# A decoder trunk on one core: the sample tile of the odd layer's input projection as unrounded products of raw weight slices, at the start of its column chunk

## The reference

```python
xn = _rms(x, norm_g)
q, k, v, g_c, qi, wi, ki, xq, g_x = _split(xn @ w_in, ODD_SPLITS)
```

## Time and profile before

| | |
|---|---|
| median of 3 runs | 1839.22 us (1837.75 to 1840.47) |
| the profiled execution | 1835.88 us, span 1834.3 us |
| PE busy in the span | 1749.9 us (95%) |
| DVE, ACT, POOL busy | 978.5 us (53%), 601.0 us (33%), 412.7 us (23%) |
| mean granted clock of TensorE | 0.989 |
| DMA | 237.10 MB, mean 129 GB/s |

### The profile page before, as it was taken

How to read it: one execution, slowest core, us unless ns; L and a number is a source line. 1 busy time by engine, 2 the same in 40 slices (tenths; PEclk the granted TensorE clock), 3 DMA queues, 4 the chain that set the end, 5 groups by cost and what they waited for, 6 DMA issues and landing times. The chain is left out here.

```text
span 1834.3 us, 26510 instructions
## 1 busy us (share of the span) xinstructions
PE 1749.9 (95%) x9413; PEld 1352.0 (74%) x9413; DVE 978.5 (53%) x2277; ACT 601.0 (33%) x1271; POOL 412.7 (23%) x643
## 2 busy tenths in 40 slices
PE   6999999999999999998999999999999679999999
PEld 5666788777888887886876567887777456777887
DVE  5422653233677655212541667888879665774111
ACT  3110332111122113101211346787735445553010
POOL 4301221100143452000341001211005455420000
PEclk9999999999999999999999999999999899999999
DMA  6433342545566467122222121334343775241231
GB/s 215 132 108 117 123 118 101 165 137 155 181 176 193 135 221 299 75 96 73 80 71 77 42 75 65 117 100 146 129 146 115 253 225 162 85 131 66 101 121 46
DMA packets 134765, 237.10 MB, mean 129 GB/s; under 512 B 28550, under 2 KB 61222, under 8 KB 134634
## 3 DMA queue, kind: packets, MB, share of 16 engines
q1 hardware_dynamic: 111066, 172.48, 29.0%
q0 software_dynamic: 17184, 55.85, 9.4%
q10 hardware_dynamic: 6384, 7.08, 1.1%
HBM read 169.12 MB, written 66.17 MB: 128 GB/s over the span
## 5 line engine op out<-in xcount | busy, mean ns | idle before, releaser
L1282 PE MATMUL ring_acc<-ring_w_hi,layer_xT_hi 128*128 128x512 f32 x640 | 260.8, 407 | 0.2 <-PE all_banks L1432 0.2
L1284 PE MATMUL ring_acc<-ring_w_hi,layer_xT_lo 128*128 128x512 f32 x640 | 249.9, 391 | 0.0
L1283 PE MATMUL ring_acc<-ring_w_lo,layer_xT_hi 128*128 128x512 f32 x640 | 249.7, 390 | 0.0
L2869 PE MATMUL front_acc<-front_w_hi,front_xT_hi 128*128 128x512 f32 x520 | 218.6, 420 | 10.5 <-DVE front_w_lo L3410 5.2
L2871 PE MATMUL front_acc<-front_w_hi,front_xT_lo 128*128 128x512 f32 x520 | 205.7, 396 | 0.0
L2870 PE MATMUL front_acc<-front_w_lo,front_xT_hi 128*128 128x512 f32 x520 | 205.5, 395 | 0.0
L1282 PEld LDWEIGHTS ring_acc<-ring_w_hi,layer_xT_hi 128*128 128x128 f32 x640 | 120.3, 188 | 29.5 <-issue 6.6
L1284 PEld LDWEIGHTS ring_acc<-ring_w_hi,layer_xT_lo 128*128 128x128 f32 x640 | 120.1, 188 | 26.1
L1283 PEld LDWEIGHTS ring_acc<-ring_w_lo,layer_xT_hi 128*128 128x128 f32 x640 | 120.4, 188 | 25.4 <-issue 2.6
L2869 PEld LDWEIGHTS front_acc<-front_w_hi,front_xT_hi 128*128 128x128 f32 x520 | 98.6, 190 | 43.3 <-issue 11.8
L3195 ACT ACTIVATE front_index_rows<-odd_bias,front_candidate 128x1024 bf16<-128x1024 f32 (+3 forms) x128 | 124.9, 981 | 9.0 <-DVEq L3559 5.1
(11 more groups left out here) (715 smaller groups left out, 3585.6 us busy)
## 6 DMA issues: line engine op xcount, KB each, us to landing
all_w<-in_w_even POOLq DMA_DIRECT2D x80, 256.0 KB, 3.8
h_even<-layer_st SPq DMA_DIRECT2D x79, 256.0 KB, 2.1
all_w<-in_w_odd POOLq DMA_DIRECT2D x61, 256.0 KB, 3.5
h_odd<-front_st SPq DMA_DIRECT2D x55, 256.0 KB, 2.1
layer_scratch<-h_even SPq DMA_DIRECT2D x46, 256.0 KB, 3.0
all_scratch<-in_w_mem SPq DMA_DIRECT2D x32, 256.0 KB, 3.6
all_scratch<-h_even SPq DMA_DIRECT2D x32, 256.0 KB, 3.6
all_scratch<-x SPq DMA_DIRECT2D x14, 512.0 KB, 3.9
```

What stands on the lines that cost most here:

```text
L1282: T.matmul(out[0:rows, :], xh[:, kk, to], wh[:, r, :], start=(kk == 0), stop=False)
L1283: T.matmul(out[0:rows, :], xh[:, kk, to], wl[:, r, :], start=False, stop=False)
L1284: ins = T.matmul(out[0:rows, :], xl[:, kk, to], wh[:, r, :], start=False, stop=(kk == KC - 1))
L2869: T.matmul(out[0:rows, :], xh[:, k, to], wh[:, r, :], start=(k == 0), stop=False, skip_group_check=True)
```

## The change

In chunks 2 to 7 the sample tile is no longer made from the split weights. It is made from the raw slices and an unrounded fp32 copy of the sample rows (`x_smp`), as four products of 128 columns for each slice, each into its own group of 32 PSUM partitions, so that the tile is 128 x 128 and not 32 x 512. As only four slices are raw at a time, it is made in two halves. Slices 0 to 3 of the next chunk are taken in the middle of unit j = 3 of the chunk before, into the bank of the unit before it, and ACT copies that sum to `hold`. Slices 4 to 7 are taken in the unit j = 0 of the chunk itself; DVE adds the two halves. So the order of tiles in chunks 2 to 7 becomes sample, 0, ..., 7 (`ORDERS`). The loads of raw slices wait until the products have read them. Chunks 0 and 1 stay as they were.

```diff
+        ORDERS = [list(range(T1)), list(range(B - 1)) + [B, B - 1]] + [[B] + list(range(B))] * (len(ORDER) - UNROUNDED)
+        tile_at = lambda chunk, j: ORDERS[chunk][j]
+        in_parts = lambda n: n == 2 * T1 - 2
+        of_sample = lambda n: n >= UNROUNDED * T1 and n % T1 == 0
+        by_dve = lambda n: ORDER[n // T1][1] or in_parts(n) or of_sample(n)
...
 # POOL, load_w(q)
+                was, k = divmod(q - RAW, KC)
+                if was >= UNROUNDED:
+                    pool.wait_ge(*((smp_mm, was - UNROUNDED + 1) if k < RAW else (mm, T1 * was + 1)))
...
 # PE
+            def sample(chunk, part, out):
+                for k in range(RAW * part, RAW * part + RAW):
+                    from_, there = slice_in(KC * chunk + k)
+                    pe.wait_ge(*there)
+                    for g in range(4):
+                        ins = T.matmul(out[32 * g:32 * g + SMP, 0:P], x_smp[:, k, :], from_[:, P * g:P * g + P],
+                                       start=(k % RAW == 0), stop=(k % RAW == RAW - 1))
+                return ins
+
             def half(n, side):
...
                 if side == 0:
...
+                    if j == HALF_AT + 1 and UNROUNDED <= chunk + 1 < len(ORDER):
+                        pe.wait_ge(held, chunk + 1 - UNROUNDED + 1)
+                    if of_sample(n):
+                        sample(chunk, 1, out).then_inc(mm, 1)
...
+                elif j == HALF_AT and UNROUNDED <= chunk + 1 < len(ORDER):
+                    pe.wait_ge(*evacuated(n - 1))
+                    sample(chunk + 1, 0, psD[(n + 1) % 2]).then_inc(smp_mm, 1)
+                if of_sample(n):
+                    if (n, side) in second_pairs:
+                        next(pairs)
+                    return
...
-                    if j == 0:
+                    if j == (1 if chunk >= UNROUNDED else 0):
                         pe.wait_ge(split_d, q + 1)
...
 # ACT, dense(n)
+                if n % T1 == HALF_AT and UNROUNDED <= chunk + 1 < len(ORDER):
+                    if chunk >= UNROUNDED:
+                        act.wait_ge(*evacuated(T1 * chunk))
+                    act.wait_ge(smp_mm, chunk + 1 - UNROUNDED + 1)
+                    A(hold[:, :], psD[(n + 1) % 2][:, 0:P], ACT.Copy, scale=0.5 if ORDER[chunk + 1][1] else 1.0).then_inc(held, 1)
...
 # DVE, dense(n)
-                if in_parts(n) and ORDER[chunk][1]:
-                    acc = psD[n % 2][0:SMP, :]
-                    dve.wait_ge(parts, part(n))
-                    V.tensor_tensor(acc, acc, st_of(n)[0:SMP, :], ALU.add).then_inc(whole, 1)
+                if of_sample(n):
+                    acc = psD[n % 2][:, 0:P]
+                    dve.wait_ge(mm, n + 1)
+                    dve.wait_ge(held, chunk - UNROUNDED + 1)
+                    if ORDER[chunk][1]:
+                        V.scalar_tensor_tensor(acc, acc, 0.5, hold[:, :], ALU.mult, ALU.add).then_inc(whole, 1)
+                    else:
+                        dve.wait_ge(*stored_by(n - ST))
+                        V.tensor_tensor(st_of(n)[:, 0:P], acc, hold[:, :], ALU.add).then_inc(ev_v, 1)
```

More of the change, by code:

```diff
@@ L2382, in layer1_front @@
         Q = s.sb("index_rows", [P, 5 * TOK])
-        xh, xl = (s.sb(n, [P, KC, TOK + SMP], F32R) for n in ("xT_hi", "xT_lo"))
+        xh, xl = (s.sb(n, [P, KC, SEQ], F32R) for n in ("xT_hi", "xT_lo"))
         wh, wl = (s.sb(n, [P, RING, CW], F32R) for n in ("w_hi", "w_lo"))
+        xs_parts = s.sb("xT_smp_hi_lo", [P, KC, 2 * SMP], F32R)
+        x_smp, hold = s.sb("xT_smp", [P, KC, SMP]), s.sb("first_half", [P, P])
         raw = c.raw
@@ L2446, in layer1_front @@
             s.sem("evacuated_by_dve"), s.sem("tanhs"), s.sem("stored", ST))
-        parts, whole, ia_in = s.sem("sample_parts"), s.sem("sample_whole"), s.sem("idx_pages_by_act_in", PAGED)
+        smp_mm, held, whole, ia_in = s.sem("first_halves"), s.sem("first_halves_held"), s.sem("sample_whole"), s.sem("idx_pages_by_act_in", PAGED)
         x_in, small_in, wk_d, wkd, rope_in = (s.sem("x_in", 2), s.sem("small_in"),
@@ L2473, in layer1_front @@
         FIRST_TILES = (0, TILES)
-        BOTH = slice(SEQ, TOK + SMP)
+        UNROUNDED, HALF_AT = 2, 3
         def slice_in(q):
@@ L2484, in layer1_front, with tanhs_to @@
         st_of = lambda n: c.vals[1][:, 0, :] if n == UNITS - 1 else st[(n - T1) % ST]
-        tile_at = lambda chunk, j: j if chunk == 0 or j < T1 - 2 else 2 * T1 - 3 - j
-        in_parts = lambda n: n >= T1 and n % T1 == T1 - 2
-        by_dve = lambda n: ORDER[n // T1][1] or in_parts(n)
+        ORDERS = [list(range(T1)), list(range(B - 1)) + [B, B - 1]] + [[B] + list(range(B))] * (len(ORDER) - UNROUNDED)
[3 more added lines that the diff above has]
+        by_dve = lambda n: ORDER[n // T1][1] or in_parts(n) or of_sample(n)
         def part(n):
-            return sum(ORDER[m // T1][1] for m in range(2 * T1 - 2, n + 1, T1))
+            return sum(ORDER[m // T1][1] for m in range(UNROUNDED * T1, n + 1, T1))
+        def tanhs_to(n):
+            return sum(ORDER[m // T1][1] or in_parts(m) for m in range(n + 1))
         def evacuated(n):
@@ L2501, in stored_by @@
             return stored[m % ST], 16 * (m // ST + 1)
-        unit_of = lambda chunk, t: T1 * chunk + tile_at(chunk, t)
+        unit_of = lambda chunk, t: T1 * chunk + ORDERS[chunk].index(t)
         def own_rows(g):
@@ L2841, in half @@
                 rows, to, out = rows_in(t), cols_in(t), psD[n % 2]
+                upper = lambda k: xh[:, k, to] if t < B else xs_parts[:, k, 0:SMP]
+                lower = lambda k: xl[:, k, to] if t < B else xs_parts[:, k, SMP:2 * SMP]
                 if side == 0:
@@ L3092, in dense @@
                 m = n - T1
+                if of_sample(n) and not ORDER[chunk][1]:
+                    return
                 if m >= ST:
@@ L3095, in dense @@
                 if in_parts(n):
-                    ins = A(st_of(n)[0:SMP, :], psD[n % 2][SMP:2 * SMP, :], ACT.Copy)
-                    if not ORDER[chunk][1]:
-                        ins.then_inc(tanhs, 1)
-                        return
-                    ins.then_inc(parts, 1)
+                    A(st_of(n)[0:SMP, :], psD[n % 2][SMP:2 * SMP, :], ACT.Copy).then_inc(tanhs, 1)
+                elif of_sample(n):
                     act.wait_ge(whole, part(n))
-                if by_dve(n):
+                    A(st_of(n)[:, 0:P], psD[n % 2][:, 0:P], ACT.Tanh).then_inc(tanhs, 1)
+                elif by_dve(n):
                     A(st_of(n)[0:rows, :], psD[n % 2][0:rows, :], ACT.Tanh).then_inc(tanhs, 1)
@@ L3353, in finished @@
                 rows = rows_in(t)
-                dve.wait_ge(tanhs, evacuated(n)[1])
-                v = st_of(n)[0:rows, :]
+                if of_sample(n) and not ORDER[chunk][1]:
+                    return
+                dve.wait_ge(tanhs, tanhs_to(n))
+                v, acc = (t[:, 0:P] if of_sample(n) else t[0:rows, :] for t in (st_of(n), psD[n % 2]))
                 if not ORDER[chunk][1]:
-                    V.tensor_tensor(v, v, psD[n % 2][0:SMP, :], ALU.add).then_inc(ev_v, 1)
+                    V.tensor_tensor(v, v, acc, ALU.add).then_inc(ev_v, 1)
                 else:
-                    V.scalar_tensor_tensor(v, v, 1.0, psD[n % 2][0:rows, :], ALU.add, ALU.mult).then_inc(ev_v, 1)
+                    V.scalar_tensor_tensor(v, v, 1.0, acc, ALU.add, ALU.mult).then_inc(ev_v, 1)
             def dense(n):
```

33 lines of the change are left out of this document (18 added, 15 removed).

## The result

| | median of the runs | profiled execution |
|---|---|---|
| before | 1838.49 us (1836.49 to 1840.47, 4 runs) | 1835.88 us, span 1834.3, clock 0.989 |
| after | 1860.58 us (1858.80 to 1868.18, 4 runs) | 1858.96 us, span 1857.4, clock 0.982 |

The changed kernel is slower: ratio 1.0128, 95% interval 1.0107 to 1.0148, some 23 us.

The account below looks back on a forecast made before the run. PE paces nearly every unit, DVE close behind. Places and products sum to +7.5 us, the clock to +5.9: +13.4 on the profiled 1835.9 us makes 1849.3, and 3.3 more for the median 1852.6 us; range 1841 to 1861.5.

Parts of the forecast that it names:

- The clock: PE's clock halves behind longer waits at the starts of chunks 4, 5, 6 and in chunk 2: +5.9 us in all.
- Chunk 2: Start of chunk 2, index pairs: the wait for ACT's relus stays, unit 19 starts at 1036.0, 2.1 us won.
- Chunk 6: Start of chunk 6: PE idles about 5 us for DVE's page copy, nothing won; j = 3's 1.2 us hidden.
- Products: Sample tile on PE: halves of 1.2 us replace tiles of 3.68 us, 7.7 us less work.
- The rival in which the groups don't overlap: Column groups of the halves run one after another, 3.7 us a half: +22 us, 1875 us; chance 0.04.
- Chunks 4, 5, 6: nothing of the 4.3 us won: At these starts PE waits 5.5, about 4.9 and about 5 us; only 0.8 us given back, at chunk 4.
- Chunk 5: Start of chunk 5: PE waits about 4.9 us for the cached page, loaded behind DVE's last multiply; nothing won.
- Chunk 3: Start of chunk 3: PE starts some 3.7 us earlier, then waits 1.3 us for `hold`; +0.1 us beyond j = 3.
- The end: Chunk 7, from unit 61: DVE's chain sets the end and the last evacuation comes 2.7 us earlier.
- The gain is kept: Rival: DVE copies as early as PE wants, so all 4.3 us are won at each start; 1831.5 us, chance 0.11.
- Partly caught up: Rival: half of each wait at three starts won, 2.1 us each, no clock loss there; +1.2, 1840.4 us, chance 0.09.
- turns the sign: Remark at chunk 4: keeping the gain needs DVE's copy 4.5 us earlier, and half of that would turn the sign.

Follow-up runs that it names:

- run 4: Changed kernel plus useless products in the sample units of chunks 4 to 6, ahead of the sample's own products; 1859.91 us, ratio 1.0110.
- run 5: Changed kernel plus useless products in chunks 2 to 6, in chunks 3 to 6 behind the sample's own products; 1856.52 us, ratio 1.0088.
- run 12: Changed kernel plus useless products in the sample unit of chunk 2 alone; 1858.74 us, ratio 1.0110.
- run 3: Changed kernel with DVE's splits of slices 4 to 7 of chunks 2 to 7 moved behind the sample unit step's other work; 1847.58 us, ratio 1.0060.
- runs 9, 11: Changed kernel with second halves made a chunk earlier, ahead of tile 7: 1843.36 us, 1.0021; the same at the steps of the kernel before: 1840.94 us, 1.0007.
- run 10: Changed kernel with only SyncE's loads of the first two cached pages moved ahead, to tile 6 of the memory attention; 1858.79 us, ratio 1.0115.
- run 8: Kernel before with only the splits of slices 4 to 7 of chunks 3 to 5 moved from j = 8 to j = 0; 1850.57 us, ratio 1.0065.

## Why the prediction was right in kind and wrong in size

The failed step is the part "The clock": "I take 2.3 us lost behind the first, 2.0 behind the second, 0.8 behind the third [...] and 0.8 in chunk 2". The mechanism is right. The term was mis-sized: 5.9 us in the sum, and the runs with useless products show 2.8 (chunk 4, run 4), 2.2 (chunk 5, run 5), 2.8 (chunk 6, run 4) and 4.3 (chunk 2, run 12), 12.1 us together. That is 6.2 of the 9.7 us missed. Each of the four is the best filling of its place; run 5, which filled all four at once, won 8.8 us in them (1.7, 2.0, 2.2 and 2.9), so by that run alone it is 2.9 of the 9.7. A second, smaller step is one that the forecast put at nothing: the store behind DVE's new add, which holds up SyncE's queue for 1.5 us at chunk 5.

- *Chunk 2.* The forecast worked out the new spacing of the pairs, 1.1 us of products and 1.2 of wait, and both are in the row to 0.1 us, but at full clock. It gave the clock 0.8 us. Yet the wait that it named as growing to 3.5 us (measured: 3.80) is of the size of the one that had dropped the clock in chunk 3 (3.63). It also measured its gain against 1038.18 us, the start of unit 19 in the kernel before; that execution was at half clock for 3.4 us just ahead of it, so some 1.5 of the 2.1 us that it forecast as won are the clock of one execution. At half clock each of three pairs takes 1 us longer, and unit 19 another 1.7.
- *Chunk 6.* The forecast cut the loss to 0.8 "where PE would wait for DVE anyway". It did not: filling the wait brought all 2.8 us back. The price of one clock loss, 2.8 us from the earlier trace rows, was good at chunks 4 and 6; the discounts taken from it were not.
- *Products.* A half is 1.08 us on its row, forecast 1.2 with its effect on neighbours. The halves at j = 3 cost 1.0 to 1.2 where no wait fell in the same unit, the full tiles at j = 7 1.7 to 1.8. The rival in which the groups don't overlap is out. The 81 ns a product of the Trainium skill ("TensorE: Matmul & The Clock Gate", "Back-to-back issue gap") is not borne out for these groups: 1.08 us for 32 records is 34 ns.
- *Chunks 4, 5, 6: nothing of the 4.3 us won.* Right, and shown from both sides: the waits stood at 5.3, 6.8 and 5.3 us (forecast 5.5, 4.9, about 5), and shrank to 0.6 us with the splits moved (chunk 4 in run 3) or to at most 1.2 us at chunk 4 with a full tile first (runs 9, 11). At chunk 4 the value without clock, -0.8, is that of run 4 to the tenth, which is luck: run 5 had 0.0.
- *Chunk 5.* Besides the clock 2.4 us were missed. 1.5 of them are SyncE's hold-up behind the sample tile's store, read from the trace; run 10 shows only that 2.8 us of the stretch hang on the page's load, clock included.
- *Chunk 3.* The wait for `hold` came (1.4 us, forecast 1.3), in this chunk only, and the stretch was 0.9 us better than forecast. What failed lies ahead of it: unit 29 started 4.5 us earlier against unit 26, not 3.7, although a wait of 3.5 us stood before it again, now for DVE's add of the sample tile, with the half clock of 6.8 us behind it. The forecast moved that evacuation to DVE and gave it no wait. Why the two together come out better is open.
- *The end.* -1.8 instead of -2.7 us, and 0.6 us more in the back. Neither was tried by itself, and the back varied by more than that between profiles.
- *The gain is kept*, the rival on the other side, is ruled out for this place. "Partly caught up" too: of the waits at chunks 4 to 6 nothing was won back. The recorded remark that half of this gain "turns the sign" does not fit its own numbers, as the next rival works half of each wait out at +1.2 us.
- *The range.* The terms given for its upper end, 1852.6 + 5.3 + 2.4, add up to 1860.3 us, not 1861.5. The measured 1860.58 lies between the two; that the stated range holds it is luck.

What stays open: 0.9 us of chunk 5's miss, chunk 3's 0.9, the 1.5 us behind unit 61, and how much between 2.9 and 6.2 us the clock term was short.

## What to carry to other kernels

A short unit belongs where the engine that runs it is alone in setting the pace. Put first in a chunk of this kernel, where DVE still had four splits and its other work to do, it turned its whole gain into a wait at three of six starts. Such a wait has to be priced twice, as idle time and as half clock behind it, in full for each wait that is as long as one that has dropped the clock before. The length alone does not settle the short ones: behind the same wait of 1.66 us the clock fell in the kernel before and stayed full in run 8. And every engine that is given a new evacuation has a queue behind it: look what the queue that stores the result holds next.

## What the hardware showed that was not expected

- Useless products can be a gain: 20 products of 512 columns in a wait of 5.3 us made the stretch 2.8 us shorter (run 4), 21 of them 2.0 us (run 5).
- The half clock began while PE still waited, 2.5 us before the wait's end at chunk 4 and 0.3 us at chunk 6. It lasted 6.8 us at both, where work without gaps followed, and 13.7 us in chunk 2, where PE ran three times for 2.08 us, with waits of 1.17 us between.
- A whole sample tile as 64 records in four column groups took 1.88 us, 29 ns a record.
